# First attention of a three-block transformer kernel: bias inside the keys, output product among the heads, split weights in another order, identity turns before six norms' products

## The reference, cut to what matters

```python
q = rms_norm(q.reshape(B, S, FOX_HEADS, HEAD_DIM), fox_g_q[j])   # 12 heads of 64
k = rms_norm(k.reshape(B, S, FOX_HEADS, HEAD_DIM), fox_g_k[j])
log_f = jax.nn.log_sigmoid((f_logit + fox_b_f[j]).astype(jnp.float32))
mix = forget_attention(q, k, v, log_f)
# in forget_attention, with c = cumsum(log_f), causal:
#   s = q.k * scale + (c[query] - c[key]); p = softmax(s); out = p.v
mem_out = memory_attention(mq, mk, mv, g_mq[i], g_mk[i])          # 4 heads
h = h + jnp.concatenate([mix, mem_out], axis=-1) @ w_out          # w_out: 1024 x 1024
z = rms_norm(h, norm_ffn[i])
h = h + swiglu(z, ffn_w_gate[j], ffn_w_up[j], ffn_w_down[j])
```

## Time and profile before

| what | us |
|---|---|
| median of the runs (lowest to highest) | 1903.74 (1902.96 to 1905.18) |
| the profiled execution | 1904.53 |
| its span | 1902.7 |
| TensorE busy | 1805.3 (95%) |
| VectorE, ScalarE, POOL busy | 1444.6, 1171.7, 204.0 |
| chain that ended last, share of TensorE | 85% |
| granted TensorE clock, mean | 0.983 |

### The profile page before, as it was taken

One profiled execution on the slowest core, in us unless ns is written; L12 is line 12 of the kernel. 1 busy time (PEld: TensorE's weight loads), 2 busy tenths in 40 slices (PEclk: granted clock), 3 DMA queues, 4 the chain that ended last, 5 costly groups with the idle time before them and its releaser, 6 DMA issues.

```text
span 1902.7 us, 27558 instructions
## 1 busy us (share of the span) xinstructions
PE 1805.3 (95%) x10598; PEld 1586.1 (83%) x10598; DVE 1444.6 (76%) x1321; ACT 1171.7 (62%) x1141; POOL 204.0 (11%) x161
## 2 busy tenths in 40 slices
PE   6988999999899999999999999999999999689997
PEld 6977999998778878788787887888877888589997
DVE  6765877777768888888888888888889854765554
ACT  5435443456657777777778777787776734743332
POOL 2033111111020000000000000000015000403221
PEclk8999999999999999999999999999999999999999
DMA  9604688841159999999999999999999934035540
GB/s 395 238 23 145 237 336 328 318 175 45 67 190 382 380 361 383 356 389 381 365 383 365 386 383 360 382 368 386 376 367 411 368 114 141 1 130 181 178 155 23
DMA packets 74571, 520.84 MB, mean 274 GB/s; under 512 B 8064, under 2 KB 8192, under 8 KB 13952
## 3 DMA queue, kind: packets, MB, share of 16 engines
q1 hardware_dynamic: 73056, 514.02, 71.0%
q0 software_dynamic: 1440, 5.77, 0.8%
HBM read 504.02 MB, written 15.73 MB: 273 GB/s over the span
## 4 chain that ended last, share of the span: by engine, by line
PE 85%; DVE 6%; ACT 5%; issue 2%; POOL 1%; DMA 0%; ACTq 0%; DVEq 0%; SPq 0%
PE ps L1160 25%; PE ps L1162 25%; PE ps L1161 25%; DVE wl L1675 2%; PE ps L1362 2%; PE ps L1183 1%; ACT wh L1034 1%; PE ps L1530 1%; DVE big L1668 1%; PE ps L1291 1%; PE ps L1312 1%; ACT L1045 0%; ACT L1034 0%; PE ps L1174 0%; DVE nmx L1834 0%
## 5 line engine op out<-in xcount | busy, mean ns | idle before, releaser
L1675 DVE TENSOR_TENSOR wl<-raw,wh 128x2048 fp32r<-128x2048 f32 x446 | 1026.6, 2305 | 294.3 <-ACT wh L740 169.9
L1034 ACT ACTIVATE wh<-raw 128x2048 fp32r<-128x2048 f32 x336 | 643.1, 1918 | 180.4 <-PE ps L1162 180.3
L1160 PE MATMUL ps<-wh,xh 128*128 128x512 f32 (+1 forms) x1040 | 398.3, 383 | 8.9 <-DVE wl L1675 8.9
L1162 PE MATMUL ps<-wh,xl 128*128 128x512 f32 (+1 forms) x1040 | 390.6, 376 | 0.0
L1161 PE MATMUL ps<-wl,xh 128*128 128x512 f32 (+1 forms) x1040 | 390.3, 375 | 0.0
L1160 PE MATMUL ps<-xh,wh 128*128 128x256 f32 x1184 | 345.2, 292 | 25.0 <-DVE xl L1675 11.4
L1161 PE MATMUL ps<-xl,wh 128*128 128x256 f32 x1184 | 340.4, 287 | 0.0
L1162 PE MATMUL ps<-xh,wl 128*128 128x256 f32 x1184 | 340.1, 287 | 0.0
L740 ACT ACTIVATE wh<-raw 128x2048 fp32r<-128x2048 f32 x107 | 204.2, 1910 | 174.9 <-PE ps L1162 171.1
L1160 PEld LDWEIGHTS ps<-xh,wh 128*128 128x128 f32 x1184 | 232.7, 196 | 30.2 <-issue 23.8
L1160 PEld LDWEIGHTS ps<-wh,xh 128*128 128x128 f32 x1040 | 196.0, 188 | 49.8 <-DVE wl L1675 15.7
(11 more groups left out here) (292 smaller groups left out, 1936.5 us busy)
## 6 DMA issues: line engine op xcount, KB each, us to landing
raw<-in_experts SPq DMA_DIRECT2D x336, 1024.0 KB, 6.9
raw<-in_units SPq DMA_DIRECT2D x134, 1024.0 KB, 5.1
x_rows<-big SPq DMA_DIRECT2D x1, 6144.0 KB, 34.6
big<-x_rows SPq DMA_DIRECT2D x8, 512.0 KB, 8.2
y_rows<-big SPq DMA_DIRECT2D x7, 512.0 KB, 8.1
y_rows<-big SPq DMA_DIRECT2D x1, 2560.0 KB, 40.6
big<-in_mem SPq DMA_DIRECT2D x1, 1024.0 KB, 7.0
hT<-in_x SPq DMA_DIRECT2D x1, 1024.0 KB, 9.0
```

What stands on the lines that cost most here:

```text
L1034: act.activation(wh[:, p % SPL, :], raw[:, n % RAW, :], ACT.Copy).then_inc(sem("hi_ready"), 1)
L1160: mm(out_, lh, rh, start=start, stop=False, **kw)
L1162: return mm(out_, ll, rh, start=False, stop=stop, **kw)
L1675: return V.tensor_tensor(out_, whole, leading.bitcast(F32), ALU.subtract)
```

## The change

- **Bias row.** The row of minus c of each head is written by two DMAs into the unused half of `kz`, where the queries have a one (`qT` for even heads and the new `q_odd` for odd heads; POOL sets zeros and ones). The matmuls of L1294 and `selh` are gone.
- **Order of units.** `PROJ` puts queries, keys and values of the first heads first. `fv1` is the last unit ahead of the attention, `fv2` is worked off in two halves beside maps 0 and 2 (`last_values`). `fox_ready` and `values_ready` wait for the parts of the projections when a head first needs them.
- **Output rows.** `fo` is stored by rows of its input (`units_by_rows`), and `fo_rows(g)`, 24 products for pair g, runs in step 2g+6 between the turns and pv; the last one follows the loop. The splits of `fv1, fv2, fo0, fo1, fo2` places are at steps 4, 7, 10, 14, 18.
- **ScalarE** copies the turned map before the exponentials of the step (`turned_first`), and the pairs are one step earlier (`out_lag=PV_LAG`). All turned maps use bank 2 and all pairs bank 3, so that banks 4 to 7 are there for `fo`.
- **Identity turns.** `keep_running(name, n)` issues n transposes of the identity behind a norm's sums (and behind the 12-column products `narrow` before `mq0`): 16, 16, 20, 32, 20, 20 at six places.

```diff
@@ -161,7 +161,8 @@
...
+PROJ = ["fq0", "fk0", "fv0", "fq1", "fk1", "fq2", "fk2", "fv1"]
+UNITS_A = (["mk0", "mv0", "mq0"] + PROJ + ["fv2"]
            + [f"fo{j}" for j in range(4)] + FF0_ORDER + ["mk1", "mv1", "mq1"] + CI_ORDER
            + [f"co{j}" for j in range(4)])
...
-        selh = sqz[:, 0:FOX_HEADS * P].rearrange("p (h m) -> p h m", h=FOX_HEADS)
-        negc = sqz[:, FOX_HEADS * P:FOX_HEADS * P + T]
+        q_odd = view(0, FOX // P, T, sqz)
+        negc = plan_f[:, :, :].rearrange("p a b -> p (a b)")
...
-        FOX_SPLITS = {16: ("fv0",), 20: ("fv1", "fv2")}
+        FOX_SPLITS = {4: ("fv1",), 7: ("fv2",), 10: ("fo0",), 14: ("fo1",), 18: ("fo2",)}
...
+        add_attention(fox_maps, (2,), (3,))
         for j in range(4):
-            product(f"fo{j}", j)
...
+            product(f"fo{j}", 4 + j)
...
+            wait_lo(pool, "mem0")
+            pool.wait_ge(sem("keys_zeroed"), 1)
+            pool.memset(qT[HD:P, 0:FOX // P, :], 0.0).then_inc(sem("queries_zeroed"), 1)
...
+            pool.memset(qT[HD:HD + 1, 0:FOX // P, :], 1.0).then_inc(sem("queries_one"), 1)
...
+            pool.memset(q_odd[0:HD, :, :], 0.0).then_inc(sem("queries_zeroed"), 1)
...
+            pool.memset(q_odd[0:1, :, :], 1.0).then_inc(sem("queries_one"), 1)
...
+            pool.wait_ge(sem("negc_ready"), 1)
+            pool.wait_ge(sem("rows_zeroed"), 32)
+            for odd in range(2):
+                pool.dma_start(kz[HD * (1 - odd):HD * (1 - odd) + 1, odd:FOX_HEADS:2, :],
+                               negc[odd:FOX_HEADS:2, :]).then_inc(sem("bias_rows"), 16)
...
-            for j in range(6):
-                name = UNITS_A[3 + j]
-                qk_square(2 + j, name)
-                split_after(name)
-                qk_sd(1 + j)
+            for j, name in enumerate(PROJ):
+                asked = (["mq0"] + PROJ)[j]
+                if name in QK_UNITS:
+                    qk_square(QK_UNITS.index(name), name)
+                else:
+                    values_out(name, vv[:, :, T * int(name[2]):T * int(name[2]) + T])
+                if name != "fv1":
+                    split_after(name)
+                if asked in QK_UNITS:
+                    qk_sd(QK_UNITS.index(asked))
                 if j == 0:
...
-            for j in range(3):
-                values_out(f"fv{j}", vv[:, :, T * j:T * j + T])
-                if j == 0:
-                    qk_sd(7)
...
-                    if i < n:
...
+                    if i < n and not turned_first:
+                        exponentials(a0 + i)
                     if 0 <= i - T_LAG < n:
...
+                        turned_out(a0 + i - T_LAG)
+                    if i < n and turned_first:
+                        exponentials(a0 + i)
+                    if 0 <= i - out_lag < n and (i - out_lag) % 2 == 1 and maps[a0]["kind"] != "diff":
+                        g = (a0 + i - out_lag) // 2
...
-            attention(fox_maps, lambda i: [split_after(name) for name in FOX_SPLITS.get(i, ())])
+            def beside_fox(i):
+                if i == 3:
+                    values_out("fv2", vv[:, :, 2 * T:3 * T])
+                for name in FOX_SPLITS.get(i, ()):
+                    split_after(name)
+            attention(fox_maps, beside_fox, out_lag=PV_LAG, turned_first=True)
...
                 square(hT, sqz, j)
-                if j < 3:
-                    split_after(f"fo{j}")
...
+            def keep_running(name, n):
+                claim(pe, name)
+                for _ in range(n):
+                    pe.transpose(bank(name)[:, 0:P], ident, ident)
             norm_sum(0)
+            keep_running("idle_mem0", 16)
...
+            keep_running("idle_x", 16)
             by_channels("mq0", ready=arriving("x"))
...
+            for j, name in enumerate(PROJ):
+                if name in QK_UNITS:
+                    by_channels(name)
+                else:
+                    by_tokens(name)
+                asked = (["mq0"] + PROJ)[j]
+                if asked in QK_UNITS:
+                    head_sum(QK_UNITS.index(asked))
...
-            head_sum(7)
...
+            def fox_ready(h):
+                if h == FOX_HEADS:
+                    wait_drained(pe, "mk0")
+                    wait_drained(pe, "mq0")
+                elif h < FOX_HEADS and h % 4 == 0:
+                    wait_drained(pe, f"fq{h // 4}")
+                    wait_drained(pe, f"fk{h // 4}")
+            def values_ready(h):
+                if h == FOX_HEADS:
+                    wait_drained(pe, "mv0")
+                elif h < FOX_HEADS and h % 4 == 0:
+                    wait_drained(pe, f"fv{h // 4}")
+                if h == 0:
+                    wait_drained(pe, "fk1")
...
+                        if ready:
+                            ready(i)
                         claim(pe, f"sc{a}")
                         for t, (at, nk) in enumerate(((0, T), (T, T)) if full else ((0, P), (P, T))):
-                            fox = m["kind"] == "fox"
                             ins = mm(s[:, at:at + nk], m["q"][:, P * t:P * t + P], m["k"][:, 0:nk],
-                                     start=True, stop=not fox)
-                            if fox:
-                                ins = mm(s[:, at:at + nk], selh[:, m["head"], :], negc[:, 0:nk],
-                                         start=False, stop=True)
+                                     start=True, stop=True)
                         ins.then_inc(filled(f"sc{a}"), 1)
...
                         turn(f"pT{a}", [(P * c, att_p[:, a % 3, P * o:P * o + P]) for c, o in enumerate(order)])
+                    if turned:
+                        turned(i)
                     if 0 <= i - PV_LAG < n:
...
+                        if values:
+                            values(i - PV_LAG)
...
-            pe.wait_ge(sem("keys_zeroed"), 1)
-            for name in ["mk0", "mv0", "mq0"] + UNITS_A[3:12]:
-                wait_drained(pe, name)
-            pe.wait_ge(sem("negc_ready"), 1)
-            pe.wait_ge(sem("selh_ready"), 1)
-            attention(fox_maps)
-            for g in range(8):
+            def fo_rows(g):
+                name, k = f"fo{g // 2}", g % 2
+                if g == 0:
+                    for j in range(4):
+                        claim(pe, f"fo{j}")
+                h, l = weights(name, 2)
                 wait_drained(pe, f"pv{g}")
-            for j in range(4):
-                by_channels(f"fo{j}")
+                for o in range(KT):
+                    n = slice(P * o, P * o + P)
+                    ins = exact(bank(f"fo{o // 2}")[:, T * (o % 2):T * (o % 2) + T], (h[:, k, n], l[:, k, n]),
+                                (xh[:, g, :], xl[:, g, :]), g == 0 and o % 2 == 0, g == KT - 1, skip_group_check=True)
+                    if g == KT - 1 and o in (1, 3, 5):
+                        ins.then_inc(sem("fo_out"), 1)
+                if k:
+                    ins.then_inc(sem("unit_done"), 1)
+            def last_values(t):
+                h, l = weights("fv2", KT)
+                if t == 0:
+                    claim(pe, "fv2")
+                for k in range(KT):
+                    c = slice(P * t, P * t + P)
+                    ins = exact(bank("fv2")[:, T * t:T * t + T], (xh[:, k, c], xl[:, k, c]), (h[:, k, :], l[:, k, :]),
+                                k == 0, k == KT - 1)
+                if t:
+                    ins.then_inc(sem("unit_done"), 1)
+            def beside_fox(i):
+                if i in (0, 2):
+                    last_values(i // 2)
+                if i % 2 == 0 and i >= 6:
+                    fo_rows((i - 6) // 2)
+            pe.wait_ge(sem("queries_one"), 2)
+            pe.wait_ge(sem("bias_rows"), 32)
+            attention(fox_maps, turned=beside_fox, ready=fox_ready, values=values_ready)
+            fo_rows(KT - 1)
             norm_sum(2)
+            keep_running("idle_ffn0", 20)
...
+            keep_running("idle_ln", 32)
...
+            keep_running("idle_mix2", 20)
...
+            keep_running("idle_ffn2", 20)
...
-            for j in range(6):
-                split_after(UNITS_A[3 + j])
+            for j, name in enumerate(PROJ):
+                if name != "fv1":
+                    split_after(name)
+                asked = (["mq0"] + PROJ)[j]
...
-                    V.tensor_copy(selh, ident[:, 0:FOX_HEADS].unsqueeze(2).broadcast_to([P, FOX_HEADS, P])).then_inc(
-                        sem("selh_ready"), 1)
...
-                elif j < 4:
-                    qk_scale(f"fq{j - 1}", [(qT[:, 2 * j - 2:2 * j, :], 0, P, gq8[:, 0:1])])
...
+                elif asked[:2] == "fq":
+                    two = slice(2 * int(at), 2 * int(at) + 2)
+                    qk_scale(asked, [(qT[0:HD, two, :], 0, HD, gq8[:, 0:1]), (q_odd[HD:P, two, :], HD, P, gq8[:, 0:1])])
+                elif asked[:2] == "fk":
+                    if asked == "fk0":
...
+                    keys(asked, kz, 4 * int(at), col(V_FGK))
...
```

(9 more changed lines are left out.)

102 lines of the change are left out of this document (47 added, 55 removed).

## The result

The changed kernel took 1909.39 us (median, 1906.12 to 1912.56), the kernel before 1903.18 beside it. The ratio is 1.0029, 95% interval 1.002 to 1.0037: slower by some 5.5 us (6.2 by the medians), where 1904 was forecast with a range of 1894 to 1917. Its profiled execution took 1912.56 us, the slowest of its runs, so its trace shows about 3 us more than the median.

A forecast was written before the change was run, and what follows sets the result against it. TensorE, busy 95% of the span, was taken as the bound. 1904.53 - 11.5 (identity turns) + 5.0 (output rows in the loop) + 6.2 (clock in the attention) = 1904.2, given as 1904, range 1894 to 1917.

The forecast's parts named there:

- rival A: Identity turns do not hold the clock, so only the attention's cost counts: 1915.7 us, chance .15.
- rival B: The clock stays at 1.00 in the attention: 1898.0 us, chance .25.
- part 4: First attention: two new TensorE idle times each bring a stretch at clock 0.50, 3.1 us each, +6.2, bounds 0 and 8.
- `mq0`: Identity turns ahead of `mq0`, behind 12-column products: 1.5 us at stake, .8 taken, between 0 and 1.5.
- Part 1: Attention scores: removing the bias matmuls shortens a head's scores from 1.42 to .76, worth nothing by itself.
- Part 2: Start of the attention: VectorE's first row at 113.5 instead of 114.21, with TensorE idle some 4 us.
- Part 3: Attention loop: output rows wait for `xl` at a chain's end, 8.4 us per pair, only partly hidden, +5.0.
- the recurrence: Row-by-row timing of the attention loop from 113.5: output rows start 17.8 to 75.8 later, end at 192.2.
- Part 5: Identity turns in the idle time before six norms' products delay nothing and keep the clock at 1.00: -11.5 us.
- Part 6: Bias-row DMAs, POOL's ones and zeros, waits for projections, residual parts: hidden or unchanged in length, worth nothing.
- rival C: Output rows are hidden as the order intends, at TensorE's own 6.84 us period: 1887.9 us, chance .08.
- The sign of being wrong: A stage elsewhere, feed-forward or experts, differing in length by more than a few tenths would make the forecast wrong altogether.

The follow-up runs named there:

- no_turns: The changed kernel without its identity turns, so only the first attention is changed: 1910.86 us, ratio 1.0041 to the kernel before.
- att_turns: The changed kernel with 38 identity turns ahead of head 2's scores and 34 ahead of the first output rows: 1905.28 us.
- turns_only: The kernel before with the six rows of identity turns and nothing else of the change: 1898.85 us, ratio 0.9969.
- turns_long_only: The kernel before with identity turns alone, 34 or 36 of them at mem0, ffn0, mix2 and ffn2: 1892.24 us, ratio 0.9944.
- small_splits: The changed kernel with the five splits among the heads done on 64 of 2048 columns: 1900.30 us.
- moved_only: The changed kernel with splits at steps 2, 7, 11, 15, 19 and the output rows left in place: 1902.34 us.
- best: The changed kernel with output rows one step later, splits moved, long rows of turns, and 38 turns ahead of head 2's scores: 1893.35 us.
- late_moved: The changed kernel with output rows one step later and splits at steps 2, 7, 11, 15, 19: 1893.66 us.

## Why the prediction was right, and where not

The range held the time, but it is wide enough for rival A's 1915.7 and rival B's 1898.0 both, and slower was given .22. The point, 1904, is 5.4 too low, and my likeliest case said no change where 0.29% slower was measured. The forecast's own inner range, 1900 to 1908.5, does not follow from the bounds it names (0 and 8 for part 4, 0 and 1.5 for `mq0`): they give 1897 to 1907.

**Part 1 (scores).** No run removes the bias matmuls alone, so their worth of nothing is not shown. With them gone, `no_turns` is slower, which fits it.

**Part 2 (start).** VectorE's first row came at 112.63, in an execution that was 1.2 ahead of the kernel before at 57 us, so 113.8 by the old count; 113.5 was forecast. TensorE's idle time there was 4.87, forecast 4.3.

**Part 3 (chain and splits).** The chain is shown: each pair's output rows wait for `xl`, `att_turns` has their starts within 1.6 us of the forecast ones, and moving splits and rows together gave 13.2 us where the recurrence said 12.1. As a whole the recurrence is not: for the rows' place alone it said 7.9 and 5.7, and 3.1 and 0.5 were measured. It had neither the clock nor the wait for the pairs' one bank; what each took is not parted. Its period also writes 3.98 where the chain's own sum is 3.93, which is worth nothing. From the first row of VectorE to the end the recurrence had 78.7 without the clock. The measured 85.5 less what the clock cost (below) is 78.

**Part 4 (clock in the attention).** Forecast: two stretches, 3.1 each, 6.2. Measured with both removed: 4.5 for the two, and a third and a fourth stretch behind the idle times of 2.48 and 3.06, which I had put into the upper bound only, about 1.5 each (1.5 measured for the fourth, the third taken as the same). The sum, some 7.5, lies between my 6.2 and my bound of 8. That B would leave the clock alone was wrong.

**Part 5 (turns).** This step failed, by its size: 5.0 and not 11.5. The price of the stretches was about right (11.5 forecast; with long rows 10.7 us by the ratio 0.9944, 12.4 by the medians, with the luck named above). What was wrong is the duration of a turn and what I concluded from it. I took .143 from three turns of data; a row of identity turns took 2.35 / 20 = .117. 20 of them fill 2.35 of 4.3 us and not 2.9, and I had read "shorter than the idle time" as "delays nothing", not as "leaves 2 us in which the clock can still fall", as it did at 13 of 36 places. At `mq0`, where .8 was forecast, the stretch is as long as before. The earlier trace rows should have been asked how much of each idle time has to be filled.

**Part 6 (edits at nothing).** No wait for the bias rows or the ones shows: TensorE goes from the last head sum into the first scores without idle time in the changed kernel.

**The sum again.** With part 5 at -5.0: 1904.5 + 11.2 - 5.0 = 1910.7, against 1909.4. That it comes so near is in part luck: the attention costs 12.1 in the trace with turns, 9.6 in that without, and 7.0 by the medians. Rival A was wrong in its mechanism (`turns_only`, `turns_long_only`), and rival C did not come, for the reason given against it.

**The sign of being wrong.** A stage elsewhere that differs by more than a few tenths was to mean that the forecast is wrong altogether. The third block's attention does differ, by 2.3 us, and its two stretches at 0.50 are what the traces show for it. The forecast took the clock outside the edited places as fixed, and it is not; a part of any difference of a few us here may come from that.

## What to carry to other kernels

Where a busy engine's clock falls behind an idle time that cannot be removed, fill the idle time up to its end, and count the filler by its own measured duration; half a filling gave less than half the gain here, and not at the same places in each kernel. Do not judge by one place in one trace. Work that is interleaved with a latency chain has to stand behind the instruction that starts the next link, not between the two, and a 2 us operation put among 0.3 us ones costs by the step at which it stands: moving four of five splits by a step or two was worth 7 us. Before an attention loop is rearranged, look at how evenly its engine is busy, since the same work with longer gaps ran in part at half the clock.

## What the runs showed of the hardware that I had not expected

An idle time of 2 to 3 us decided nothing by its length here. The 2.11 us in the first attention were followed by 0.50 in `turns_only` and by 1.00 in the kernel before and in `turns_long_only`; 2.17 us ahead of the sixth output rows were followed by 0.50 in `small_splits` (at 171.69) and by 1.00 in `moved_only` (at 173.36); and the 2.48 us of the changed kernel (at 161.54) stand in `no_turns` too (at 160.12), where the clock stays at 1.00 behind them. Three idle times of 1.3 to 1.7 us in a row ended in a stretch at 0.50 in `best` (122.1 to 128.9).

A turn of the identity, back to back, took .114 to .119 us, and a plain fp32 product of the same shape twice that, with no better effect on the clock for the same time.

One kernel spreads over 3 to 9 us from run to run (1906.12 to 1912.56 for the changed one, 1893.15 to 1902.27 for `late_moved`), and the clock goes with it: the fastest run of `late_moved` has a mean clock of 0.990, the slowest 0.984.
